# Queues by kind for waiting VectorE work, a new order of the first loads and folds, and the MLP scale on x instead of W1

## The chip, the cores and the metric

The kernel runs on the 8 NeuronCores of one Trainium2 chip, without collectives: each core computes half of the 32 tiles of 128 tokens of one batch element. The metric is the device time of the slowest core in microseconds (us). The engines are TensorE (PE, matmuls into PSUM), VectorE (DVE), ScalarE (ACT, the exp), GpSimd (POOL, which also issues the weight loads) and SyncE (SP, which issues the other transfers).

## The reference

One decoder block on x of 4 x 4096 x 1024, cut to what matters:

```python
xn = rmsnorm(x, norm_mix_g)
u = xn @ w_in                              # conv gates and values, q, k, v, branch gates
y_a = short_gated_conv(b_g, c_g, v_a, conv_w) @ w_a_out    # causal, 3 taps
# 4 heads, two softmax maps each, ALiBi bias, causal:
p = softmax(q k^T / 8 + bias)              # (B, H, 2, 128, S)
o = (p[:, :, 0] - lam * p[:, :, 1]) @ v
y_b = (rmsnorm(o, subln_g) * (1 - lam_init)) @ w_b_out
x = x + (sigmoid(g_a) * y_a + sigmoid(g_b) * y_b) @ w_o
h = rmsnorm(x, norm_mlp_g) @ w_mlp_in
x = x + square(relu(h)) @ w_mlp_out
return rmsnorm(x, norm_final_g)
```

## The kernel before

A core owns 16 query tiles in four groups (g = 0 to 3) of 512 tokens, and needs K and V of all 4096 tokens, in eight blocks of 512 (blocks 0 to 3 are its own, 4 to 7 the other core's). The program is written as one list per engine: each recorded operation goes to the end of its engine's list and waits for what it reads and overwrites, so **the order in which the Python code records is the order in which each engine works**, and an engine that waits holds up everything behind it. A tile that is one buffer is waited for as a whole.

*Start.* POOL issues the loads of Wk and x of block 4 in four pieces, four token tiles of block 4 (`tok_pool`, the tensor `xs`), Wv, x of block 0 and Wq. `fold_gain` multiplies Wk, Wv and Wq by the norm's gain on VectorE. `stats` computes a block's 1/rms: four squares on ScalarE, then `rstd` (VectorE, POOL's power, VectorE). `bcast` spreads 1/rms of a block over all partitions by TensorE and copies it to the tile `R`, which scales Q, K of blocks 1 to 3, and the normalised x.

*Attention.* `pairs` holds the (group, head, key tile) steps: 4 heads of 4, 8, 12 and 16 steps. Step n issues the scores of step n+1 (`qk`, TensorE), their exp (`ex`, ScalarE, on the diagonal also two masks on VectorE), then P V of step n in two halves (`pv`). After each half `other` does one round of other work: it calls `run_deferred`, which takes waiting VectorE operations from the queue `bg`, and then, while `credit` is above zero, takes chunks from the list `W`. A chunk is a projection of 8 matmuls of 512 columns into PSUM bank 7, the only bank that chunks have here, and its evacuation; its weight is taken off the credit (0.5 per half step). The weights stand in `W`: 1 for a projection, 0 for a load or a statistics step. At a change of group `until(g)` runs all of `W` up to that group's mark at once.

*Waiting work.* `background` puts VectorE operations into `bg` with a tag: "conv" (four operations between the second and third projection of a convolution chunk, `fv` and `fb`), "head" (ten after a head: 1/l, differences, norm), "norm" (eight, which normalise x of a block in place, and a spill), "fold". `settle(tag)` records, at once, everything up to the last operation of that tag, in the order in which it came. `epilogue` at a head's end settles "head", then copies the accumulators out of banks 4 and 5 by VectorE and of bank 6 by ScalarE.

*End.* Gates and output projection (`G_list`) of the four groups, from x normalised, then the MLP in four blocks of 512 tokens: `m_load` transposes x from memory into `m_x2` (two buffers), 32 `m_in` chunks fill `h2`, eight `m_out` chunks add to x. W1 is scaled by the MLP norm's gain in 64 VectorE operations ("fold") while the last group's attention and the gates run.

The functions that the change touches, and what calls them:

## Time and profile before

| | us |
|---|---|
| median of 3 runs | 1317.37 (1315.82 to 1317.42) |
| profiled execution, its own time | 1320.41 |
| its span, first to last instruction, slowest core | 1318.9 |
| spans of the 8 cores | 1307.3 to 1318.9 |
| TensorE busy in the span | 1171.4 |
| VectorE, ScalarE, POOL busy | 487.3, 543.0, 89.7 |

The profile is of one execution on its slowest core. An engine's busy time says little by itself: what counts is, stage by stage, which wait ends last. TensorE's granted clock is 1 at 2.4 GHz and 0.5 at 1.2 GHz, and a mean over a stretch lies between.

### The profile page before, as it was taken

What the parts mean: (1) busy time and instruction counts of PE and PEld (TensorE: products, weight loads), DVE (VectorE), ACT (ScalarE), POOL (GpSimd) and SP (SyncE); (2) the same over time, 40 slices, a digit from 0 to 9 for tenths busy, and PEclk for the clock granted to TensorE, in tenths of its full rate; (3) what the DMA queues carried; (4) which work ended last, traced back from release to release, by engine and by line L of the source; (5) the groups of instructions that cost most, each with busy time, mean ns of one, the idle gap of its engine ahead of it and who ended that gap; (6) DMA issues with size and microseconds to landing.
All of it is one profiled execution on the core that took longest, in us unless ns stands there. A gap on an engine that the chain in (4) does not pass through costs nothing.

```text
span 1318.9 us, 20312 instructions; the slowest of 8 cores (1307.3 to 1318.9 us)
## 1 busy us (share of the span) xinstructions
PE 1171.4 (89%) x7010; PEld 560.4 (42%) x7010; DVE 487.3 (37%) x1107; ACT 543.0 (41%) x744; POOL 89.7 (7%) x148
## 2 busy tenths in 40 slices
PE   3886677987898898897889899999999999999996
PEld 1333243443454344453445344444444444444442
DVE  2446454445434554325252464432122122122212
ACT  1263265656656467675667132233023113212300
POOL 3111100000000000100000000020000000000000
PEclk8888888998899899999899999999999999999998
DMA  9965612313012551654613757099313013012001
GB/s 175 228 157 97 132 65 65 70 36 68 18 29 45 109 109 32 105 109 118 144 33 69 197 127 239 10 214 170 104 50 78 16 49 97 0 48 80 1 32 48
DMA packets 67412, 117.75 MB, mean 89 GB/s; under 512 B 37072, under 2 KB 39376, under 8 KB 66288
## 3 DMA queue, kind: packets, MB, share of 16 engines
q0 software_dynamic: 14544, 44.11, 20.7%
q1 hardware_dynamic: 52768, 72.34, 18.1%
q8 instruction: 59, 0.97, 0.3%
q14 instruction: 41, 0.34, 0.1%
HBM read 120.69 MB, written 29.36 MB: 114 GB/s over the span
## 4 chain that ended last, share of the span: by engine, by line
PE 78%; DVE 9%; DMA 4%; issue 4%; ACT 3%; POOL 1%; DVEq 0%; SPq 0%; ACTq 0%; POOLq 0%
PE ps_all L404 78%; ACT big L664 2%; DMA big<-wv 2%; DMA big<-xs 2%; DVE big L793 1%; DVE big L689 1%; DVE big L492 1%; DVE big L549 1%; POOL big L409 1%; DVE big L611 1%; DVE big L604 0%; DVE big L602 0%; POOL big L723 0%; DVE big L715 0%; DVEq L152 0%
## 5 line engine op out<-in xcount | busy, mean ns | idle before, releaser
L404 PE MATMUL ps_all<-big 128*128 128x512 bf16 (+2 forms) x7010 | 1171.4, 333 | 135.0 <-DVE big L611 24.1
L404 PEld LDWEIGHTS ps_all<-big 128*128 128x128 bf16 (+1 forms) x7010 | 560.4, 100 | 745.5 <-issue 284.1
L664 ACT ACTIVATE big<-ps_all,big 128x1024 bf16<-128x1024 f32 (+3 forms) x384 | 339.0, 926 | 167.3 <-PE ps_all L404 158.9
L889 ACT ACTIVATE big<-ps_all 128x512 bf16<-128x512 f32 x128 | 76.2, 597 | 134.0 <-PE ps_all L404 133.6
L890 DVE TENSOR_TENSOR big<-big 128x512 bf16<-128x512 bf16 x128 | 54.4, 425 | 152.6 <-ACT big L889 152.1
L906 ACT ACTIVATE big<-big 128x1024 bf16<-128x1024 f32 x16 | 16.9, 1057 | 208.3 <-DVE big L901 208.3
L901 DVE SCALAR_TENSOR_TENSOR big<-ps_all,big 128x512 f32<-128x512 f32 x32 | 24.0, 751 | 162.9 <-PE ps_all L404 162.9
L793 DVE SCALAR_TENSOR_TENSOR big<-big,ps_all 128x512 f32<-128x512 f32 x64 | 43.7, 686 | 97.0 <-PE ps_all L404 96.6
L782 ACT ACTIVATE big<-ps_all,big 128x512 f32<-128x512 f32 x64 | 43.5, 686 | 58.9 <-PE ps_all L404 57.0
L448 ACT ACTIVATE big<-big 128x1024 bf16<-128x1024 f32 x32 | 33.8, 1056 | 47.4 <-DMA big<-xs 46.8
L821 ACT ACTIVATE big<-big 128x1024 bf16<-128x1024 f32 x16 | 16.9, 1057 | 71.9 <-DVE big L816 71.9
L669 DVE TENSOR_TENSOR big<-big 128x256 bf16<-128x256 bf16 x64 | 18.6, 290 | 61.6 <-ACT big L664 61.1
L816 DVE SCALAR_TENSOR_TENSOR big<-ps_all,big 128x512 f32<-128x512 f32 x32 | 22.1, 691 | 50.1 <-PE ps_all L404 41.1
L549 DVE TENSOR_SCALAR big<-ps_all,big 128x512 bf16<-128x512 f32 x32 | 24.0, 750 | 44.1 <-PE ps_all L404 44.1
L908 POOL TENSOR_TENSOR big<-big 128x1 f32<-128x1 f32 x16 | 8.7, 543 | 413.5 <-DVE big L907 413.5
L409 POOL DMA_DIRECT2D big<-w x32 | 17.4, 550 | 280.4 <-PE ps_all L404 167.9
L595 DVE TENSOR_TENSOR big<-ps_all,big 128x512 f32<-128x512 f32 x16 | 11.0, 690 | 49.7 <-PE ps_all L404 49.7
L671 DVE TENSOR_SCALAR big<-big 128x256 bf16<-128x256 bf16 x64 | 18.3, 286 | 29.2 <-ACT big L664 29.1
L723 POOL TENSOR_TENSOR big<-big 128x4 f32<-128x4 f32 x16 | 16.4, 1024 | 175.2 <-DVE big L721 175.1
L1051 DVE TENSOR_SCALAR big<-big 128x512 bf16<-128x512 bf16 x64 | 22.5, 352 | 4.3 <-DVE big L1051 0.9
L707 DVE SCALAR_TENSOR_TENSOR big<-big 128x128 f32<-128x128 f32 x64 | 22.3, 349 | 4.5
L796 DVE TENSOR_TENSOR big<-big 128x512 bf16<-128x512 f32 x32 | 22.1, 692 | 3.3
(65 smaller groups left out, 308.1 us busy)
## 6 DMA issues: line engine op xcount, KB each, us to landing
big<-xs SPq DMA_DIRECT2D x40, 512.0 KB, 9.1
big<-w POOLq DMA_DIRECT2D x32, 512.0 KB, 10.6
xm_sp<-big SPq DMA_DIRECT2D x16, 512.0 KB, 5.6
big<-xm_sp SPq DMA_DIRECT2D x16, 512.0 KB, 5.2
out<-big SPq DMA_DIRECT2D x16, 512.0 KB, 2.6
big<-xT POOLq DMA_DIRECT2D x24, 256.0 KB, 5.1
big<-xs POOLq DMA_DIRECT2D x8, 512.0 KB, 20.4
xn_sp<-big SPq DMA_DIRECT2D x4, 1024.0 KB, 4.5
```

What stands on the lines that cost most here:

```text
L404: S.op("pe", lambda e: e.matmul(out, lhsT, rhs, start=start, stop=stop, skip_group_check=skip), reads, writes)
L409: S.dma("pool", lambda e: e.dma_start(out=dst, in_=src), writes=bufs, extra=[S.last["pe"]] if paced else (), part=part)
L448: act(lambda e: e.activation(junk.ap, xt.ap, AF.Square, accum_out=ss1[blk].ap[:, t:t + 1]), [xt], [junk, ss1[blk]])
L549: dve(lambda e: e.tensor_scalar_mul(v_all[:, :, n, 0:128], ps.rearrange("p (h v) -> p h v", h=4), rs1[blk].ap[:, t:t + 1]), [key, rs1[blk] ...
L664: act(lambda e, a=a, b=b, c=c, s=s, PT=PT, scale=scale: e.activation(PT.ap[:, :, a:b], Sb[s][:, :, a:b], AF.Exp, bias=ccol(C_BTAB + c), sc ...
L707: dve(lambda e, t=t: e.scalar_tensor_tensor(o[:, 0, t, 0:128], o[:, 0, t, 0:128], rl[:, 0, t:t + 1], o[:, 1, t, 0:128], ALU.mult, ALU.add) ...
L782: act(lambda e: e.activation(t.ap, ps, AF.Tanh, bias=hbg.ap[:, 8 * w + dm:8 * w + dm + 1], scale=0.5), [key, hbg], [t])
L793: dve(lambda e: e.scalar_tensor_tensor(t.ap, t.ap, 1.0, ps, ALU.add, ALU.mult), [key, t], [t])
L889: act(lambda e: e.activation(r.ap, ps, AF.Relu), [key], [r])
L890: dve(lambda e: e.tensor_tensor(h2[fc].ap, r.ap, r.ap, ALU.mult), [r], [h2[fc]])
L901: dve(lambda e: e.scalar_tensor_tensor(x.ap[:, hs], ps, r2q[b].ap[:, t:t + 1], x.ap[:, hs], ALU.mult, ALU.add), [key, x, r2q[b]], [x])
L1051: return lambda: dve(lambda e: e.tensor_scalar_mul(W1[k].ap[:, c, :], W1[k].ap[:, c, :], ccol(C_GMLP + c)), [W1[k], cst], [W1[k]])
```

## The change

- `R` gets two buffers, and the queue "norm" becomes "norm0" and "norm1" (even and odd blocks).
- `bg` is one queue per tag. `run_deferred` takes from the first that is not empty, in the order conv, head, norm0, norm1, fold; two at a time where more than 10 wait (before: more than 8). `settle(tag)` empties that queue alone.
- `epilogue` copies bank 4, bank 6, bank 5, all on VectorE.
- Start: Wv and x of block 0 are loaded before the token tiles of block 4; 40 dummy matmuls run before the first projection and 16 after it (`warm`); the folds of Wv come before the statistics of block 4; all eight folds of Wq come after K of block 0; the four Q projections of block 0 are made first and evacuated after `bcast(0)`; the statistics of block 5 and of the halo move into the attention stage.
- `bcast` of blocks 1, 2 and 3 weighs 1 (before 0.2 or 0.6), `halo_norm` 1 (0.2), a halo chunk 0.5 (0.4).
- The 64 folds of W1 go. `m_fold` scales the eight slices of `m_x2` instead, eight for block 0 in the gates of the last group, the others between the `m_out` chunks of the block before. `m_load(0)` comes 12 rounds earlier.

```diff
-    R_b = ar.take("R", [512], F32)
+    R_b = [ar.take("R%d" % k, [512], F32) for k in range(2)]
...
-            settle("norm")
+            settle("norm%d" % (blk % 2))
...
-            background("norm", [nrm(k) for k in range(8)] + [spill])
+            background("norm%d" % (blk % 2), [nrm(k) for k in range(8)] + [spill])
...
+        def out(m):
+            dve(lambda e: e.tensor_copy(o[:, m, 0:3, 0:129], bank(4 + m)[:, 0:390].rearrange(
                 "p (t e) -> p t e", t=3)[:, :, 0:129]), [pk(4 + m)], [o_raw])
-        act(lambda e: e.copy(o[:, :, 3, 0:129], bank(6)[:, 0:260].rearrange(
+        out(0)
+        dve(lambda e: e.tensor_copy(o[:, :, 3, 0:129], bank(6)[:, 0:260].rearrange(
             "p (m e) -> p m e", m=2)[:, :, 0:129]), [pk(6)], [o_raw])
+        out(1)
...
-        for k in range(2 if len(bg) > 8 else 1):
-            if bg:
-                bg.pop(0)[1]()
-
-    bg = []
+        n = sum(len(q) for q in bg.values())
+        for k in range(2 if n > 10 else 1):
+            for q in bg.values():
+                if q:
+                    q.pop(0)()
+                    break
+
+    bg = {t: [] for t in ("conv", "head", "norm0", "norm1", "fold")}
 
     def background(tag, fns):
 
-        bg.extend((tag, f) for f in fns)
-
-    def settle(tag=None):
-
-        last = [k for k, (t, f) in enumerate(bg) if tag in (None, t)]
-        for k in range(last[-1] + 1 if last else 0):
-            bg.pop(0)[1]()
+        bg[tag].extend(fns)
+
+    def settle(tag):
+
+        while bg[tag]:
+            bg[tag].pop(0)()
...
+    def m_fold(b, c):
+        if b < 4:
+            x2 = m_x2[b % 2]
+            dve(lambda e: e.tensor_scalar_mul(x2.ap[:, c, :], x2.ap[:, c, :], ccol(C_GMLP + c)), [x2, cst], [x2])
...
+    def warm(n):
+
+        for k in range(n):
+            mm(bank(7)[:, 0:256], ident, cbf.ap, True, True, [cbf], [pk(7)])
+
+
+    warm(40)
...
+    warm(16)
+    for c in range(8):
+        fold_gain(Wv, c)
...
-    W += spread(ks(0) + vs(0), [lambda c=c: fold_gain(Wq, c) for c in range(8)])
-    W[-12:-12] = [(0, f) for f in stats(0, 5)]
-    W += [(0.2, bcast(0))]
-    W += spread(qs(0), xT_steps(1, 0) + stats(5, 1))
+    W += [(1, f) for f in ks(0)] + [(0, lambda: [fold_gain(Wq, c) for c in range(8)])]
+    W += [(0, f) for f in stats(0, 5)] + [(1, f) for f in vs(0)]
+
+    def q_first():
+        ps = [q_mm(0, h) for h in range(4)]
+        bcast(0)()
+        for h in range(4):
+            q_evac(0, h, *ps[h])
+    W += [(4, q_first)] + [(0, f) for f in xT_steps(1, 0)]
     mark(0)
-    W += spread(ks(5) + vs(5), stats(1, 2) + normed(0) + wc_load(0))
-    W += [(0.2, bcast(1))]
+    W += spread(ks(5) + vs(5), stats(5, 1) + [halo_stat] + stats(1, 2) + wc_load(0) + normed(0))
+    W += [(1, bcast(1))]
...
-    W += [(0.2, halo_norm)] + [(0.4, halo_chunk(ch)) for ch in range(4)]
-    W += spread(conv(0), normed(1) + stats(6, 3))
-    W += [(0.6, bcast(2))]
+    W += [(1, halo_norm)] + [(0.5, halo_chunk(ch)) for ch in range(4)]
+    W += spread(conv(0), stats(6, 3) + normed(1))
+    W += [(1, bcast(2))]
...
-        def fold(k):
-            def one(c):
-                return lambda: dve(lambda e: e.tensor_scalar_mul(W1[k].ap[:, c, :], W1[k].ap[:, c, :],
-                                                                 ccol(C_GMLP + c)), [W1[k], cst], [W1[k]])
-            return lambda: background("fold", [one(c) for c in range(8)])
...
-    deferred.append((36, lambda: m_load(0)))
+    deferred.append((24, lambda: m_load(0)))
+    deferred.append((48, lambda: background("fold", [lambda c=c: m_fold(0, c) for c in range(8)])))
...
             m_out(b, t, 0)
+            m_fold(b + 1, 2 * t)
             if pend:
                 m_fin2(pend.pop(0))
             if t + 2 < 4:
                 m_xload(T + 2)
             m_out(b, t, 1)
+            m_fold(b + 1, 2 * t + 1)
```

What this does to the order of work shows best on VectorE. In the rows below, `ps_all` is PSUM, `big` is the one SBUF tensor from which all tiles are cut, and x2 means that the row comes twice in a row. The first place is the second `bcast`, in the attention of the first group. Before (line 492 normalises x of block 0, 689 are copies at a head's end, 549 an evacuation of V, 669 and 671 masks, 484 the copy to `R`, 531 K times `R`):

```order
L492 SCALAR_TENSOR_TENSOR big<-big 128x512
L689 COPY big<-ps_all 128x3x129 x2
L492 SCALAR_TENSOR_TENSOR big<-big 128x512 x2
L549 TENSOR_SCALAR big<-ps_all,big 128x4x128
L669 TENSOR_TENSOR big<-big 128x2x128
L671 TENSOR_SCALAR big<-big 128x2x128
L492 SCALAR_TENSOR_TENSOR big<-big 128x512 x4
L484 COPY big<-ps_all 128x512
L531 TENSOR_TENSOR big<-ps_all,big 128x512
```

And after, at the same `bcast` (696 and 699 copies at a head's end, 705 to 724 the head's waiting operations, 551 V, 675 and 677 masks, 484 the copy to `R`, 533 K times `R`):

```order
L696 COPY big<-ps_all 128x3x129
L699 COPY big<-ps_all 128x2x129
L696 COPY big<-ps_all 128x3x129
L705 RECIPROCAL big<-big 128x8
L706 TENSOR_SCALAR big<-big 128x4
L551 TENSOR_SCALAR big<-ps_all,big 128x4x128
L675 TENSOR_TENSOR big<-big 128x2x128
L677 TENSOR_SCALAR big<-big 128x2x128
L709 TENSOR_TENSOR big<-big 128x4x128
L716 SCALAR_TENSOR_TENSOR big<-big 128x128 x2
L484 COPY big<-ps_all 128x512
L716 SCALAR_TENSOR_TENSOR big<-big 128x128 x2
```

The eight normalising operations (L492 before) are no longer ahead of the copy to `R`; what stands there is work of the head that has just ended, including the third copy, 128x2x129, which ScalarE made before.

The second place is a convolution chunk in the attention of the second group. Before (595 is `fv`, 599 to 604 the convolution between the projections, 611 `fb`, the evacuation at the chunk's end; 700 to 728 the head's operations, 721 and 728 behind POOL's power and product):

```order
L700 TENSOR_TENSOR big<-big 128x4x128
L707 SCALAR_TENSOR_TENSOR big<-big 128x128 x2
L595 TENSOR_TENSOR big<-ps_all,big 128x4x128
L707 SCALAR_TENSOR_TENSOR big<-big 128x128 x2
L715 SCALAR_TENSOR_TENSOR big<-big 128x128 x4
L721 TENSOR_SCALAR big<-big 128x4
L728 TENSOR_TENSOR big<-big 128x512
L599 COPY big<-big 128x4x2
L601 TENSOR_SCALAR big<-big 128x512
L602 SCALAR_TENSOR_TENSOR big<-big 128x512
L604 SCALAR_TENSOR_TENSOR big<-big 128x512
L611 TENSOR_TENSOR big<-ps_all,big 128x512
```

And after (601, 605 to 610 and 617 are the same operations of the convolution, 709 to 724 those of the head):

```order
L709 TENSOR_TENSOR big<-big 128x4x128
L716 SCALAR_TENSOR_TENSOR big<-big 128x128 x2
L601 TENSOR_TENSOR big<-ps_all,big 128x4x128
L605 COPY big<-big 128x4x2
L607 TENSOR_SCALAR big<-big 128x512
L608 SCALAR_TENSOR_TENSOR big<-big 128x512
L610 SCALAR_TENSOR_TENSOR big<-big 128x512
L617 TENSOR_TENSOR big<-ps_all,big 128x512
L716 SCALAR_TENSOR_TENSOR big<-big 128x128 x2
L724 SCALAR_TENSOR_TENSOR big<-big 128x128 x2
```

Between `fv` and `fb` stood the whole rest of the head; now only the four operations of the convolution do, and the head's follow `fb`.

The third place is the boundary between the first and the second block of the MLP. Before (901 are evacuations of `m_out`, 907 and 912 the final norm, 890 the square in an `m_in` chunk):

```order
L901 SCALAR_TENSOR_TENSOR big<-ps_all,big 128x512
L912 SCALAR_TENSOR_TENSOR big<-big 128x1024
L901 SCALAR_TENSOR_TENSOR big<-ps_all,big 128x512
L907 TENSOR_SCALAR big<-big 128x1
L890 TENSOR_TENSOR big<-big 128x512 x5
L912 SCALAR_TENSOR_TENSOR big<-big 128x1024
L890 TENSOR_TENSOR big<-big 128x512 x27
```

And after (917 evacuations of `m_out`, 890 now `m_fold`, 923 and 928 the final norm, 906 the square of `m_in`):

```order
L890 TENSOR_SCALAR big<-big 128x512
L923 TENSOR_SCALAR big<-big 128x1
L917 SCALAR_TENSOR_TENSOR big<-ps_all,big 128x512
L890 TENSOR_SCALAR big<-big 128x512
L928 SCALAR_TENSOR_TENSOR big<-big 128x1024
L917 SCALAR_TENSOR_TENSOR big<-ps_all,big 128x512
L890 TENSOR_SCALAR big<-big 128x512
L923 TENSOR_SCALAR big<-big 128x1
L906 TENSOR_TENSOR big<-big 128x512 x5
L928 SCALAR_TENSOR_TENSOR big<-big 128x1024
L906 TENSOR_TENSOR big<-big 128x512 x27
```

A fold now follows each evacuation of `m_out`; the last one, after the last evacuation, writes the tile that the first `m_in` matmul of the next block reads. On TensorE the change adds 56 dummy matmuls of 128x256 at the start and moves the Q projections of block 0 together.

## Rows read from the trace of the kernel before

**Rows 1.** Windows by stage: busy us of each engine (instructions), granted TensorE clock, DMA share, GB/s.

```profile
0.00:70.60 70.60, 44.62 (x172) 17.85 (x172) 23.23 (x56) 15.27 (x26) 18.26 (x37) 0.88 0.96 200
...
70.60:731.00 660.40, 555.77 (x4212) 284.92 (x4210) 293.34 (x729) 398.36 (x502) 50.84 (x74) 0.93 0.37 80
...
871.00:1319.00 448.00, 435.40 (x2018) 197.16 (x2015) 101.02 (x195) 95.28 (x162) 10.28 (x19) 0.99 0.27 66
```

**Rows 2.** What TensorE waited for: total us, times, longest us.

```profile
PE ps_all L404 <- DVE big L611: 24.1, 8, 4.7
```

**Rows 3.** Windows, columns as above: one after the halo, one after a head's end.

```profile
159.00:176.00 17.00, 11.51 (x128) 7.13 (x129) 5.61 (x23) 8.78 (x16) 1.04 (x1) 0.60 0.39 128
...
397.00:402.00 5.00, 3.47 (x17) 1.49 (x16) 2.03 (x6) 1.61 (x2) 0.00 (x0) 0.66 0.18 32
```

**Rows 4.** Timeline of the start: start us, us, operation, count, idle before it and releaser.

```profile
36.95 1.14 DVE L524 TENSOR_SCALAR big<-big 128x512 bf16<-128x512 bf16 x4 [1.55 <-DMA big<-wv]
...
56.14 1.06 ACT L448 ACTIVATE big<-big 128x1024 bf16<-128x1024 f32 x1 [0.73 <-DMA big<-xs]
...
58.97 0.69 DVE L529 CAST big<-ps_all 128x512 bf16<-128x512 f32 x1
...
59.57 0.35 DVE L524 TENSOR_SCALAR big<-big 128x512 bf16<-128x512 bf16 x1
...
60.69 0.74 DVE L549 TENSOR_SCALAR big<-ps_all,big 128x512 bf16<-128x512 f32 x1
...
64.38 0.68 DVE L484 COPY big<-ps_all 128x512 f32<-128x512 f32 x1
...
65.23 0.69 DVE L561 TENSOR_TENSOR big<-ps_all,big 128x512 bf16<-128x512 f32 x1 [0.17 <-PE ps_all L404]
...
70.61 4.52 ACT L664 ACTIVATE big<-ps_all,big 128x512 bf16<-128x512 f32 x6 [2.51 <-PE ps_all L404]
```

**Rows 5.** Timeline of the start: POOL's issues of four `xs` loads, and VectorE beside them.

```profile
5.87 2.18 POOL L409 DMA_DIRECT2D big<-xs  x4
...
33.90 2.16 POOL L409 DMA_DIRECT2D big<-xs  x4
...
34.15 1.25 DVE L524 TENSOR_SCALAR big<-big 128x512 bf16<-128x512 bf16 x4
```

**Rows 6.** Timeline at a convolution chunk of the second group.

```profile
208.45 0.69 DVE L728 TENSOR_TENSOR big<-big 128x512 bf16<-128x512 f32 x1 [1.32 <-POOL big L723]
...
211.72 0.69 DVE L611 TENSOR_TENSOR big<-ps_all,big 128x512 bf16<-128x512 f32 x1 [0.17 <-DVE big L604]
...
212.56 0.81 PE L404 MATMUL ps_all<-big 128*128 128x512 bf16 x3 [4.03 <-DVE big L611]
```

**Rows 7.** Timeline of TensorE at the second `bcast`.

```profile
111.99 1.44 PE L404 MATMUL ps_all<-big 128*128 128x512 bf16 x3 [2.17 <-DVE big L484]
```

**Rows 8.** Timeline of TensorE where the second group's first halo chunk starts.

```profile
162.39 0.59 PE L404 MATMUL ps_all<-big 128*128 128x32 bf16 x16 [6.10 <-DVE big L519]
```

**Rows 9.** Timeline of TensorE in the chunks run ahead of the second group.

```profile
144.59 1.89 PE L404 MATMUL ps_all<-big 128*128 128x512 bf16 x8 [1.01 <-DVE big L549]
```

**Rows 10.** Timeline at the end of a head of the third group.

```profile
394.59 0.56 DVE L689 COPY big<-ps_all 128x387 f32<-128x387 f32 x1
...
396.03 0.37 ACT L691 COPY big<-ps_all 128x258 f32<-128x258 f32 x1 [1.74 <-DVE big L689]
...
397.15 0.69 DVE L700 TENSOR_TENSOR big<-big 128x512 f32<-128x512 f32 x1
...
398.59 1.86 PE L404 MATMUL ps_all<-big 128*128 128x512 bf16 x4 [1.53 <-DVE big L561]
```

**Rows 11.** The page, part 5, and VectorE's timeline at the end of an MLP block.

```profile
L1051 DVE TENSOR_SCALAR big<-big 128x512 bf16<-128x512 bf16 x64 | 22.5, 352 | 4.3 <-DVE big L1051 0.9
...
974.99 0.75 DVE L901 SCALAR_TENSOR_TENSOR big<-ps_all,big 128x512 f32<-128x512 f32 x1 [4.96 <-PE ps_all L404]
```

**Rows 12.** Timeline of TensorE at a head's end in the fourth group.

```profile
610.14 2.40 PE L404 MATMUL ps_all<-big 128*128 128x512 bf16 x6 [4.70 <-DVE big L793]
```

More of the change, by code:

```diff
@@ L530, in k_evac @@
         else:
[L531 removed]
+            r = R_b[blk % 2]
+            dve(lambda e: e.tensor_tensor(dst.ap, ps, r.ap, ALU.mult), [key, r], [dst])
     def k_chunk(blk, h):
@@ L552, in v_chunk, with q_mm, q_evac @@
         return f
-    def q_chunk(g, h):
-        def f():
-            x = XT[slot_of[g]]
-            ps, key = obank()
-            for c in range(8):
-                mm(ps, Wq[c].ap[:, h * 128:(h + 1) * 128], x[c].ap, c == 0, c == 7, [Wq[c], x[c]], [key])
-            dst = qt_of[g % 2][h]
-            dve(lambda e: e.tensor_tensor(dst.ap, ps, R_b.ap, ALU.mult), [key, R_b], [dst])
-        return f
+    def q_mm(g, h):
+        x = XT[slot_of[g]]
+        ps, key = obank()
+        for c in range(8):
+            mm(ps, Wq[c].ap[:, h * 128:(h + 1) * 128], x[c].ap, c == 0, c == 7, [Wq[c], x[c]], [key])
+        return ps, key
+    def q_evac(g, h, ps, key):
+        dst, r = qt_of[g % 2][h], R_b[g % 2]
+        dve(lambda e: e.tensor_tensor(dst.ap, ps, r.ap, ALU.mult), [key, r], [dst])
+    def q_chunk(g, h):
+        return lambda: q_evac(g, h, *q_mm(g, h))
     def halo_chunk(ch):
@@ L943, in build_program @@
     slot_of[4], slot_of[0], slot_of[5] = 0, 1, 2
-    for t in range(4):
-        tok_pool(4, t)
     for q in range(2):
@@ L949, in build_program @@
         wload(XT[1], xT_d[0], 4 * q, 4, 512)
+    for t in range(4):
+        tok_pool(4, t)
     for q in range(2):
@@ L963, in build_program @@
         k_evac(4, h, *ps4[h])
+    warm(16)
+    for c in range(8):
+        fold_gain(Wv, c)
     for f in stats(4, None):
@@ L969, in build_program @@
         wload(XT[2], xT_d[5], 4 * q, 4, 512)
-    for c in range(8):
-        fold_gain(Wv, c)
     def wc_load(ch):
@@ L999, in build_program @@
     W += spread(conv(1), xT_steps(3, 1) + stats(7, None))
-    W += [(0.6, bcast(3))]
+    W += [(1, bcast(3))]
     W += spread(ks(3) + vs(3) + qs(3), xT_steps(7, 0))
@@ L1047, in w1_steps @@
             out += pieces([W1[k]], w1_d, 4096 * k, 4096)
-        def fold(k):
-            def one(c):
-                return lambda: dve(lambda e: e.tensor_scalar_mul(W1[k].ap[:, c, :], W1[k].ap[:, c, :],
-                                                                 ccol(C_GMLP + c)), [W1[k], cst], [W1[k]])
-            return lambda: background("fold", [one(c) for c in range(8)])
-        return [(2 + 4 * n, f) for n, f in enumerate(out)] + [(26 + 4 * n, fold(2 * h + n)) for n in range(2)]
+        return [(2 + 4 * n, f) for n, f in enumerate(out)]
     def w2_load(f0, n):
@@ L1098, in build_program @@
     run_deferred(True)
-    settle()
+    for t in bg:
+        settle(t)
     w2_load(0, 18)
```

14 lines of the change are left out of this document (6 added, 8 removed).

## The prediction

> **What bounds the kernel now.** I first read the windows by stage, to see where TensorE is not working. In the MLP it is busy 435.4 of 448.0 us at a granted clock of 0.99: nothing to win there but its end [rows 1]. The attention stage (70.6 to 731 us) is busy 555.8 of 660.4 us at a mean clock of 0.93, so 104.6 us are idle, and the clock takes more. With two levels of clock (1.2 and 2.4 GHz), a mean of 0.93 over the busy time costs 0.07 x 555.8 = 38.9 us. VectorE is busy for 293 us of that stage and ScalarE for 398, so neither is full: TensorE waits for an engine that does the wrong thing first, not for one with too much to do. The start (0 to 70.6 us) is different: the DMA engines are busy 0.96 of it.
>
> Next I read the list of what TensorE waited for. Its longest line is the evacuation that ends a convolution chunk, 24.1 us in eight waits, one of them 4.7 [rows 2]. Last I read the granted clock behind such waits: it is 0.60 in the 17 us after the halo and 0.66 in the 5 us after a head's end [rows 3]. The chip lowers the clock after TensorE has stood, so each long wait is paid a second time.
>
> **The start.** The Wv load moves ahead of the four `xs` loads of block 4; the bytes and the queue are the same, so the last load that the first exp needs, `xs` of block 0, should still arrive at about 56 us [rows 4]. The chain behind it is VectorE's: from 58.97 it runs two K casts (0.69), then four V evacuations with six folds of Wq in between (0.74 and 0.35), and reaches the copy of `R` at 64.38; then each Q chunk is evacuated as TensorE makes it, and the first exp starts at 70.61 [rows 4]. In the changed order the casts and folds stand ahead of the statistics, and the 32 Q matmuls ahead of the copy of `R`. What is left behind 58.97 is four V evacuations at a pitch of 0.66 (0.74 less some 0.08, as neighbours overlap: the fold at 59.57 starts 0.60 after a cast of 0.69), the copy 0.68, one Q evacuation 0.69 and some 0.5 us to the exp: 58.97 + 2.6 + 0.7 + 0.7 + 0.5 = 63.5, a gain of 7.1. The cover is TensorE's: V of block 4, K, V and Q of block 0 are 128 matmuls, some 28 us at the full clock (435.4 us / 2018 in the MLP is 0.216 each [rows 1]), and Wv arrives earlier than the 36.95 of the row. (The 2.1 MB that it passes are 10 us at the 200 GB/s of [rows 1]; I take 6, as the other loads are under way at the same time.) So they end near 60. The dummy matmuls cost nothing: 40 run before the first weights are there, 16 in a stretch in which TensorE waited for Wv anyway. If the clock is low through half of these matmuls they end 6 us later and the gain is about 2; without any wait it is 9. I take 7.
>
> Here a rule speaks against the change. The issue of four `xs` loads by POOL took 2.18 us with VectorE nearly idle and 2.16 us with four bf16 folds of 1.25 us running beside it [rows 5]. So the eight folds of Wq in one block, beside which POOL issues loads, cost those loads nothing that the row shows. The Trainium skill, page "SBUF — State Buffer", section "SBUF: two separate sides", says that a DMA issued from POOL cannot have its descriptors written while VectorE runs in a two-port mode. By that rule those issues would wait for the folds, and this trace does not show it. What it would give is among the rivals.
>
> **The queues.** Before, a convolution chunk that is settled drags every head operation queued ahead of it onto VectorE: in the row, the normalisation that waits for POOL (208.45) and the four convolution operations run before the evacuation at 211.72, and TensorE stands 4.03 us [rows 6]. After, the convolution operations go first and the head's follow the evacuation. What stays of each of the eight waits is about the evacuation and its hand-over, 0.69 + 0.2: 24.1 - 8 x 0.9 = 17 us [rows 2, 6]. The work is not gone, it is moved behind; the next place it could be late is the following head's end, four or more pairs on. Bounds: 10, if diagonal pairs still hold VectorE for their masks, and 22. The second and fourth `bcast` no longer wait for eight normalising operations, as `R` has two buffers: TensorE stood 2.17 us for the copy [rows 7], twice is 4 (2 to 6).
>
> **The halo.** TensorE stood 6.10 us in front of the first halo chunk, which shares a slot with `halo_norm` and needs its result [rows 8]. With a slot of its own, pair work comes between; an ordinary head's end still costs about 3, so 3.2 is won (1.5 to 6). The larger weights also leave about one more chunk each to be run ahead at the start of the second and third group, where one bank is shared and TensorE stands 1.01 us per chunk [rows 9]: minus 2 (0 to 3).
>
> **The head's end.** Before, two copies, ScalarE's copy, and with more than eight operations queued both the reciprocal and the 0.69 us product stand before the chunk's evacuation, for which TensorE stands 1.53 us [rows 10]. After, VectorE does all three copies (the third is a 258-wide piece, between 0.37, ScalarE's price, and 0.56, that of 387 columns), which ends the last copy about when ScalarE's ended; the product mostly moves behind the evacuation. That is worth 0.6 at about 8 of 16 heads: 5 (0 to 10).
>
> **The MLP scale.** 64 folds of W1 at 0.352 go, 22.5 us of VectorE [rows 11]; where they stood before the head's copies and a gate's evacuation, TensorE stood 4.70 us [rows 12]. About 3 of that and 2 at two later heads: 5 (2 to 8). In their place 32 folds of x2 come. Eight are hidden behind block 3's gates, 21 of the others behind the matmuls of `m_out`, but the last of each of three blocks stands behind the last evacuation, and the next block's first matmul reads the same tile. TensorE, which runs on there now [rows 1], must wait 0.75 + 0.352 and two hand-overs, about 1.25 [rows 11]: minus 3.7 (3.3 to 5).
>
> **The clock.** Of 38.9 us I let 16 come back, those behind the waits that go (the halo's window alone holds 0.40 x 11.51 = 4.6, a head's end 0.34 x 3.47 = 1.2) [rows 1, 3]. Bounds: 6, if ordinary head ends and the groups' starts still lower it, and 30.
>
> **Sum.** 7 + 17 + 4 + 3.2 - 2 + 5 + 5 - 3.7 + 16 = 51.5 us. The profiled execution took 1320.4 us, so 1268.9; the runs' median is 3.0 lower, so I say 1265 to 1266. The lower bounds together give 15.5 (2 + 10 + 2 + 1.5 - 3 + 0 + 2 - 5 + 6), the upper 87.7.
>
> **Rivals.**
> - *The stalls move.* The chunks have one PSUM bank, and VectorE's copies, masks and evacuations are the same number; if the waits return behind the masks, 15 to 30 us are left, about 1294. For it: VectorE is only 44% busy in the stage and TensorE waits for it all the same [rows 1]. Against: in the row the late work is none that TensorE needs [rows 6].
> - *More.* If the clock stays up from the second group on, its term is 30, the head's end gives its 10 and the queues their 22: 30 - 16 + 10 - 5 + 22 - 17 = 24 more, about 1242.
> - *Slower.* ScalarE's copy is put on the engine that TensorE waits for at every head's end [rows 10]. If it is fully exposed, 0.43 + 0.17 x 16 heads is 9.6 us, and if then every head end lowers the clock as in [rows 3], another 16 x 1.2 = 19, together 29. It decides from the point where the queues, `bcast` and clock give back less than 20 of their 37 and the head's end nothing: the rest is 7 + 3.2 - 2 + 5 - 3.7 = 9.5. With none of the 37, the time is up to 1337; I say 1325.
> - *It does not do what it says.* If the queues seldom hold two kinds at a time, little is reordered, and start, MLP and run-ahead nearly cancel (7 - 3.7 - 2): about 1316. The eight waits speak against.
> - *POOL held up.* If folds hold back the issues, `xs` of block 0 comes 8 x 0.35 = 2.8 us later, and the time is about 1268. This is what the page "SBUF — State Buffer" of the Trainium skill would do here.
>
> **Chances.** Forecast (35 to 75 us gained) 0.58, stalls move 0.25, more 0.08, slower 0.05, no effect 0.03, POOL 0.01. A difference of under 0.2% (2.6 us) cannot be told from none, so faster is 0.92, same 0.03, slower 0.05. For eight in ten the range takes the forecast, the lower end of "more" as far as 1240, and nearly all of the stalls that move (1287 to 1302): 1240 to 1302.
>
> **What the profile after would show.** First exp at 63 to 64 us, not after 66; TensorE's waits for the convolution's evacuation under 8 us together, none over 2; no wait of 2 us at the second `bcast`, none over 4 at the halo; the attention stage under 620 us at a clock of 0.95 or more; three new waits of 1 to 1.4 us in the MLP, at the blocks' ends. I am wrong if the idle time of the attention stage stays near 100 us, or if it falls and the clock does not rise.

## The result, and the profile after

The changed kernel takes 1285.65 us (median of 4 runs, 1285.20 to 1287.45) against 1317.39, a ratio of 0.9764 with an interval of 0.9747 to 0.9781: 2.2 to 2.5% less, about 32 us. A second set of runs of the changed kernel, the control of the experiments, has a median of 1286.05 and gave 0.9753 (0.9735 to 0.9772). The forecast was 1265 in a range of 1240 to 1302: the right sign, and 0.6 of the size.

The windows of the profiled execution of the changed kernel, split where the first exp starts, where the last one starts, and where the MLP starts (busy us of PE, PEld, DVE, ACT, POOL, then granted clock, DMA share, GB/s):

```profile
0.00:66.99 66.99, 49.55 (x226) 24.06 (x226) 21.44 (x56) 10.69 (x18) 18.31 (x37) 0.95 0.92 187
66.99:688.40 621.41, 545.71 (x4193) 284.90 (x4194) 285.55 (x697) 395.23 (x493) 51.06 (x74) 0.95 0.39 86
688.40:831.00 142.60, 136.64 (x630) 61.23 (x629) 68.74 (x123) 36.76 (x60) 10.48 (x18) 0.99 0.59 153
831.00:1283.70 452.70, 436.40 (x2020) 197.23 (x2018) 106.33 (x216) 94.15 (x160) 10.29 (x19) 0.99 0.25 65
```

And the attention stage of the trace before, cut at the same events:

```profile
70.60:726.00 655.40, 552.62 (x4193) 283.48 (x4192) 289.33 (x717) 396.83 (x500) 50.84 (x74) 0.93 0.37 80
```

Almost all of the gain lies in the attention stage: 621 us instead of 655. The start gives 3.6, the gates 3.4 (146.0 before; on the median core nothing, 140.4 before and 140.8 now), and the MLP, 446.9 before, loses 5.8 (2.6 on the median core). The clock in the attention stage is 0.95 instead of 0.93.

What TensorE waited for in the whole changed execution (us, times, longest), and five rows of the same view of before that are not shown above:

```profile
PE ps_all L404 <- DVE big L696: 16.0, 26, 2.1
PE ps_all L404 <- DVE big L804: 15.9, 20, 4.4
PE ps_all L404 <- DVE big L551: 8.4, 8, 2.3
PE ps_all L404 <- DVE big L617: 6.8, 4, 2.6
PE ps_all L404 <- DVE big L890: 3.8, 3, 1.3
PE ps_all L404 <- DVE big L699: 3.5, 13, 0.3
PE ps_all L404 <- DVE big L578: 1.4, 1, 1.4
PE ps_all L404 <- DVE big L484: 1.2, 1, 1.2
PE ps_all L404 <- DVE big L520: 0.4, 1, 0.4
```

```profile
PE ps_all L404 <- DVE big L793: 17.5, 20, 4.7
PE ps_all L404 <- ACT big L691: 9.7, 11, 0.9
PE ps_all L404 <- DVE big L689: 8.7, 10, 2.8
PE ps_all L404 <- DVE big L484: 4.5, 3, 2.2
PE ps_all L404 <- DVE big L572: 2.1, 2, 1.2
```

By these lists the evacuation at a convolution chunk's end (L611 before, L617 now) costs 6.8 us instead of 24.1 [rows 2]. The list names the operation that ended last before TensorE went on, and that is not always the one that it waited for. In 175 of the 183 waits for VectorE in the two traces TensorE starts 0.145 to 0.148 us after the named operation ends. In the other eight it starts sooner, and each time an evacuation had ended 0.146 us before. One of them, in the changed kernel:

```profile
189.95 0.69 DVE L617 TENSOR_TENSOR big<-ps_all,big 128x512 bf16<-128x512 f32 x1 [0.17 <-DVE big L610]
190.56 0.19 DVE L705 RECIPROCAL big<-big 128x8 f32<-128x8 f32 x1
190.79 1.71 PE L404 MATMUL ps_all<-big 128*128 128x512 bf16 x4 [1.99 <-DVE big L705]
```

Here TensorE starts 0.04 us after the reciprocal and 0.15 after the evacuation, so the wait is the evacuation's. Counted so, a chunk's end costs 10.0 us in six waits instead of 27.6 in ten.

The `bcast` copy (L484) costs 1.2 us instead of 4.5; the halo (`halo_norm` L520 and the halo chunk L578 now, L519 [rows 8] and L572 before) 1.8 instead of 8.2. The copies at a head's end (L696 and L699 now, L689 and L691 before) cost 19.5 instead of 18.4: nothing was won there. The gates' evacuation (L804 now, L793 before) hardly moved, and L890, the fold of x2, is new.

For the comparisons below one table was worked out from the traces. In the attention stage (first to last exp), the distance from each matmul's start to the next is split in three: its columns at the full clock, what they take more at the granted clock, and the rest. The score matmuls have 64 rows and start in pairs 3 ns apart; a pair is counted once. At the full clock 512 columns take 0.216 us (the MLP's row [rows 1]), at the half 0.427. The rest is waiting, and also some 0.1 us before and after the score matmuls of every step, which all the kernels have; so its differences count, not its level. The numbers are medians over six cores; the other two lack some matmul records. The columns come to 458 to 459 us in every row. The runs `q1_fifo`, `h1_act`, `m1_w1fold` and `m2_early` shared a chip on which some cores ran at a lower clock, in the kernel before as well (1328.7 us there), so of these four the stages of the undisturbed cores are read (four or five in the table for the first and the third) rather than the time.

| kernel | stage | rest | lost to the clock |
|---|---|---|---|
| before | 653.7 | 162.1 | 31.6 |
| changed | 621.2 | 139.1 | 23.4 |
| changed, control | 621.6 | 139.4 | 23.8 |
| changed, one queue | 653.6 | 162.6 | 32.4 |
| before, queues alone | 632.0 | 149.0 | 22.5 |
| changed, one R | 634.8 | 148.7 | 27.1 |
| changed, old weights | 618.0 | 139.0 | 19.8 |
| changed, ScalarE's copy as before | 618.0 | 140.0 | 19.4 |
| changed, folds of W1 | 626.0 | 142.6 | 25.0 |
| changed, folds of x2 earlier | 622.2 | 139.1 | 24.3 |
| changed, old start | 618.6 | 138.0 | 20.3 |
| changed, ScalarE beside VectorE | 610.0 | 133.6 | 18.4 |
| three edits | 607.4 | 131.2 | 17.4 |

### The profile page after: what moved, and what is told of

The parts are those of the page before. It is cut to its first block, busy times and chain, and to the rows that moved or that the text cites. A ratio compares the mean times of both kernels' runs of the same rounds, so it can differ in the third digit from the quotient of the medians.

```text
span 1283.7 us, 20390 instructions; the slowest of 8 cores (1268.7 to 1283.7 us)
## 1 busy us (share of the span) xinstructions
PE 1168.3 (91%) x7066; PEld 567.4 (44%) x7066; DVE 482.1 (38%) x1091; ACT 536.8 (42%) x728; POOL 90.1 (7%) x148
## 4 chain that ended last, share of the span: by engine, by line
PE 80%; DVE 7%; ACT 4%; issue 4%; DMA 3%; POOL 1%; SPq 0%; DVEq 0%; ACTq 0%; POOLq 0%
PE ps_all L404 80%; ACT big L670 3%; DMA big<-xs 3%; DVE big L696 1%; DVE big L804 1%; ACT big L448 1%; POOL big L409 1%; DVE big L699 1%; DVE big L551 0%; DVE big L565 0%; DVE big L608 0%; DVE big L610 0%; DVE big L617 0%; SPq L836 0%; DVE big L493 0%
## 5 line engine op out<-in xcount | busy, mean ns | idle before, releaser
L404 PE MATMUL ps_all<-big 128*128 128x512 bf16 (+6 forms) x7066 | 1168.3, 331 | 102.9 <-DVE big L696 16.0
L404 PEld LDWEIGHTS ps_all<-big 128*128 128x128 bf16 (+2 forms) x7066 | 567.4, 100 | 703.3 <-issue 226.7
L804 DVE SCALAR_TENSOR_TENSOR big<-big,ps_all 128x512 f32<-128x512 f32 x64 | 43.8, 686 | 102.5 <-PE ps_all L404 102.1
L793 ACT ACTIVATE big<-ps_all,big 128x512 f32<-128x512 f32 x64 | 43.4, 685 | 59.3 <-PE ps_all L404 59.2
L409 POOL DMA_DIRECT2D big<-w x32 | 17.6, 557 | 283.5 <-PE ps_all L404 163.0
L551 DVE TENSOR_SCALAR big<-ps_all,big 128x512 bf16<-128x512 f32 x32 | 23.4, 749 | 34.1 <-PE ps_all L404 34.0
L601 DVE TENSOR_TENSOR big<-ps_all,big 128x512 f32<-128x512 f32 x16 | 11.1, 691 | 34.4 <-PE ps_all L404 34.4
L493 DVE SCALAR_TENSOR_TENSOR big<-big 128x512 bf16<-128x512 bf16 x32 | 23.0, 743 | 0.0
```

The lines of the kernel that those rows point to most:

```text
L404: S.op("pe", lambda e: e.matmul(out, lhsT, rhs, start=start, stop=stop, skip_group_check=skip), reads, writes)
L409: S.dma("pool", lambda e: e.dma_start(out=dst, in_=src), writes=bufs, extra=[S.last["pe"]] if paced else (), part=part)
L493: dve(lambda e: e.scalar_tensor_tensor(x[k].ap, x[k].ap, ccol(C_GMIX + k), r.ap, ALU.mult, ALU.mult), [x[k], cst, r], [x[k]])
L551: dve(lambda e: e.tensor_scalar_mul(v_all[:, :, n, 0:128], ps.rearrange("p (h v) -> p h v", h=4), rs1[blk].ap[:, t:t + 1]), [key, rs1[blk] ...
L793: act(lambda e: e.activation(t.ap, ps, AF.Tanh, bias=hbg.ap[:, 8 * w + dm:8 * w + dm + 1], scale=0.5), [key, hbg], [t])
L804: dve(lambda e: e.scalar_tensor_tensor(t.ap, t.ap, 1.0, ps, ALU.add, ALU.mult), [key, t], [t])
```

## The experiments

Theory: the queue is the change; without it an evacuation for which TensorE stands carries the rest of a head on its back, and the clock follows. Rival: the gain is a sum of independent parts, each about as large as the prediction has it.

**One queue again** (`q1_fifo`), on the changed kernel:

```diff
-        n = sum(len(q) for q in bg.values())
-        for k in range(2 if n > 10 else 1):
-            for q in bg.values():
-                if q:
-                    q.pop(0)()
-                    break
+        for k in range(2 if len(bg) > 8 else 1):
+            if bg:
+                bg.pop(0)[1]()
...
-        while bg[tag]:
-            bg[tag].pop(0)()
+        last = [k for k, (t, f) in enumerate(bg) if tag in (None, t)]
+        for k in range(last[-1] + 1 if last else 0):
+            bg.pop(0)[1]()
```

> The changed kernel with one queue in order of arrival again (two at a time above 8), all else kept. If the queues are the main term, as the prediction has it: TensorE's waits for the evacuation that ends a convolution chunk go from 6.8 us back to 20 or more, the clock loses some 6 us on top, and the time is 1306 to 1314 us. Rival: the gain came from the halo's slot, the second R and the order of the steps, and the order within the queue counts little: under 1294.

Measured: 1331.7 us, ratio 1.0028 (0.9995 to 1.0062), so nothing of the gain is left. That is more than the theory asked for. (The edit also takes the threshold for two at a time back from 10 to 8; the two are not told apart, here and in the next run.) The timeline of this kernel at a convolution chunk (start, length, idle before and what ended it):

```profile
304.48 0.17 DVE L730 TENSOR_SCALAR big<-big 128x4 f32<-128x4 f32 x1
304.80 1.01 POOL L732 TENSOR_TENSOR big<-big 128x4 f32<-128x4 f32 x1 [38.82 <-DVE big L730]
305.97 0.69 DVE L737 TENSOR_TENSOR big<-big 128x512 bf16<-128x512 f32 x1 [1.32 <-POOL big L732]
306.85 0.49 DVE L607 TENSOR_SCALAR big<-big 128x512 f32<-128x512 f32 x1
309.25 0.69 DVE L617 TENSOR_TENSOR big<-ps_all,big 128x512 bf16<-128x512 f32 x1 [0.17 <-DVE big L610]
310.08 2.72 PE L404 MATMUL ps_all<-big 128*128 128x512 bf16 x6 [6.63 <-DVE big L617]
```

The head's end (L730, POOL's power, L737) stands ahead of the convolution (L607 and on), VectorE itself waits 1.32 us for POOL, and TensorE stands 6.63 us for an evacuation of 0.69. On core 6 these waits make 20.8 us by the list, longest 6.7, and with three under other names 27.2 in ten waits, against 27.6 in ten before the change. In the table the rest rises by 23.2 us and the clock's loss by 8.6, together the 32 of the stage, which is back at its length before.

**The queues alone** (`p1_queues`), on the kernel before: the same lines the other way round, and

```diff
-    bg = []
+    bg = {t: [] for t in ("conv", "head", "norm", "fold")}
```

> The kernel before with the queues by kind alone (conv, head, norm, fold; two at a time above 10), all else as before. From the run with one queue, which gave back all of the gain: queues alone win about 30 us, 1285 to 1290, with the waits at the ends of the convolution chunks under 8 us. Rival, the prediction's sum (17 for these waits and a share of the clock's 16, the rest by the other parts): 1294 to 1300.

Measured: 1300.26 us, 0.9867 (0.9846 to 0.9888): 17.5 us less, the rival's value; the slowest core decides that, and the median core gains more. The stage shrinks by 21.7, 13.1 of it the rest and 9.1 clock. So the queue's part is 32 us in the attention stage when it is taken from the changed kernel, and 22 there when it is put on the kernel before. What holds it back there, in what TensorE waited for:

```profile
PE ps_all L404 <- DVE big L484: 7.1, 3, 5.5
PE ps_all L404 <- DVE big L519: 5.3, 1, 5.3
```

The wait for the `bcast` copy has grown, from 4.5 to 7.1: with convolution and head ahead of them, the normalising operations wait longer, and with one R all that are left must be done before the copy. The halo's wait is the old one, as the weights are the old ones. A third place does not show in these two rows, because the list puts it under L721:

```profile
177.93 5.38 DVE L492 SCALAR_TENSOR_TENSOR big<-big 128x512 bf16<-128x512 bf16 x8
183.23 0.68 DVE L611 TENSOR_TENSOR big<-ps_all,big 128x512 bf16<-128x512 f32 x1
184.06 1.44 PE L404 MATMUL ps_all<-big 128*128 128x512 bf16 x3 [4.31 <-DVE big L721]
```

Eight normalising operations of the next block stand ahead of a convolution chunk's last evacuation: with one queue "norm" the chunk's projection settles them, though it reads the block before. (The longest of the eight waits before, 4.7 us, has the same eight ahead of it.) With this wait and two more that the list puts under L443 the chunks' ends cost 11.1 us in six waits, not under the 8 that was expected.

**One R** (`r1_oneR`), on the changed kernel:

```diff
-    R_b = [ar.take("R%d" % k, [512], F32) for k in range(2)]
+    R_b = [ar.take("R", [512], F32)] * 2
...
-            settle("norm%d" % (blk % 2))
+            settle("norm")
...
-            background("norm%d" % (blk % 2), [nrm(k) for k in range(8)] + [spill])
+            background("norm", [nrm(k) for k in range(8)] + [spill])
...
-    bg = {t: [] for t in ("conv", "head", "norm0", "norm1", "fold")}
+    bg = {t: [] for t in ("conv", "head", "norm", "fold")}
```

> The changed kernel with one buffer R and one queue "norm", the other queues kept. The prediction's term is 4 us (two waits of 2.17): 1290. Rival, from the run with the queues alone, where TensorE stood 5.5 us at the second bcast: 6 to 10 us slower than the changed kernel, the clock behind that wait included, 1292 to 1296. Third: the normalisation is seldom still queued there, within 2 us.

Measured: 1297.02 us, 0.9838 (0.9819 to 0.9857), 11 us slower than the control: the rival. Timeline at the `bcast` of block 2:

```profile
215.33 4.72 DVE L493 SCALAR_TENSOR_TENSOR big<-big 128x512 bf16<-128x512 bf16 x7
220.22 0.69 DVE L484 COPY big<-ps_all 128x512 f32<-128x512 f32 x1 [0.17 <-DVE big L493]
221.06 1.44 PE L404 MATMUL ps_all<-big 128*128 128x512 bf16 x3 [4.51 <-DVE big L484]
```

Seven normalising operations in a row, then the copy, and TensorE stands 4.51 us. The waits for L484 are 9.5 us instead of 1.2, the clock's loss 3.3 more. Before the change this wait was 2.17 [rows 7]; with the queues by kind alone it is 5.5, and the second R is what keeps them from that.

**The old weights** (`w1_weights`):

```diff
-    W += [(1, bcast(1))]
+    W += [(0.2, bcast(1))]
...
-    W += [(1, halo_norm)] + [(0.5, halo_chunk(ch)) for ch in range(4)]
+    W += [(0.2, halo_norm)] + [(0.4, halo_chunk(ch)) for ch in range(4)]
...
-    W += [(1, bcast(2))]
+    W += [(0.6, bcast(2))]
...
-    W += [(1, bcast(3))]
+    W += [(0.6, bcast(3))]
```

> The changed kernel with the old weights (bcast 0.2 and 0.6, halo_norm 0.2, a halo chunk 0.4). The prediction's terms (halo 3.2 won, chunks run ahead 2 lost): 1.2 us slower, 1287. Rival, from the run with the queues alone (5.5 us of waiting at the halo, and a lower clock behind it): 4 to 6 us slower, 1290 to 1292, with that wait back.

Measured: 1281.91 us, 0.9722 (0.9698 to 0.9745): 4 us faster than the control, with intervals that overlap at their ends. Both expectations missed. The halo's wait is back in what TensorE waited for,

```profile
PE ps_all L404 <- DVE big L520: 5.4, 1, 5.4
```

and the stage is no longer for it: the rest is the same to 0.4 us, so the new weights pay elsewhere what they win here. By the waits that is at the chunks' ends (6.5 us with the old weights, 10.0 with the new) and at the copies of a head's end (17.2 and 19.5). The 4 us are the clock's, and the runs below show that this term moves by as much without a cause that the table names.

**ScalarE's copy as before** (`h1_act`): VectorE copies banks 4 and 5, then ScalarE bank 6.

```diff
-        out(0)
-        dve(lambda e: e.tensor_copy(o[:, :, 3, 0:129], bank(6)[:, 0:260].rearrange(
+        for m in range(2):
+            dve(lambda e, m=m: e.tensor_copy(o[:, m, 0:3, 0:129], bank(4 + m)[:, 0:390].rearrange(
+                "p (t e) -> p t e", t=3)[:, :, 0:129]), [pk(4 + m)], [o_raw])
+        act(lambda e: e.copy(o[:, :, 3, 0:129], bank(6)[:, 0:260].rearrange(
             "p (m e) -> p m e", m=2)[:, :, 0:129]), [pk(6)], [o_raw])
-        out(1)
```

> The changed kernel with ScalarE's copy of bank 6 at a head's end, behind VectorE's two, as before. The prediction's step (a head's end wins 5 us): 1290. Rival, from the two traces (waits for the copies 18.4 us before, 21.5 after): the copy on VectorE costs what it saves, and the time is 1282 to 1287; then the waits for banks 4, 5 and 6 together stay within 3 us of 21.5.

Measured: 1283.94 us; the stage is 618.0, the rest 140.0 against 139.4. The rival: the copy on VectorE wins nothing. The waits for the three banks are 20.7 us (11.6 for ScalarE's, 9.1 for VectorE's) against 19.5 in the changed kernel; the 21.5 of the expectation counts the reciprocal's 2.0, which is a chunk's end.

**ScalarE beside VectorE** (`h2_par`): ScalarE's copy is recorded first and has a dependence of its own.

```diff
+        act(lambda e: e.copy(o[:, :, 3, 0:129], bank(6)[:, 0:260].rearrange(
+            "p (m e) -> p m e", m=2)[:, :, 0:129]), [pk(6)], ["o3"])
+        for m in range(2):
+            dve(lambda e, m=m: e.tensor_copy(o[:, m, 0:3, 0:129], bank(4 + m)[:, 0:390].rearrange(
+                "p (t e) -> p t e", t=3)[:, :, 0:129]), [pk(4 + m)], [o_raw])
...
-            dve(lambda e: e.reciprocal(rl.unsqueeze(3), o[:, :, :, 128:129]), [o_raw], [est])
+            dve(lambda e: e.reciprocal(rl.unsqueeze(3), o[:, :, :, 128:129]), [o_raw, "o3"], [est])
```

> The changed kernel with bank 6 copied at a head's end by ScalarE, beside VectorE's two copies and not behind them (a dependence of its own for that piece). If TensorE waits there for the third copy in a row on VectorE: the waits for banks 4, 5 and 6 fall from 21.5 us to about 12 and the time is 8 to 14 us less than the control, 1272 to 1278. Rival: ScalarE comes late from its exps, and TensorE waits for it instead: within 2 us of the control.

Measured: 1270.86 us, 0.9649 (0.9631 to 0.9668), 13.7 us less than the control. First the timeline of the changed kernel at a head's end, then that of this one:

```profile
218.03 0.55 DVE L696 COPY big<-ps_all 128x387 f32<-128x387 f32 x1
218.73 0.33 PE L404 MATMUL ps_all<-big 128*128 128x129 bf16 x3 [1.13 <-DVE big L696]
218.75 0.43 DVE L699 COPY big<-ps_all 128x258 f32<-128x258 f32 x1 [0.17 <-DVE big L696]
219.28 0.56 DVE L696 COPY big<-ps_all 128x387 f32<-128x387 f32 x1
219.32 0.22 PE L404 MATMUL ps_all<-big 128*128 128x129 bf16 x1 [0.27 <-DVE big L699]
219.99 0.39 PE L404 MATMUL ps_all<-big 128*128 128x129 bf16 x4 [0.45 <-DVE big L696]
```

```profile
208.19 0.37 ACT L694 COPY big<-ps_all 128x258 f32<-128x258 f32 x1
209.27 0.56 DVE L697 COPY big<-ps_all 128x387 f32<-128x387 f32 x1
209.97 0.39 PE L404 MATMUL ps_all<-big 128*128 128x129 bf16 x4 [1.14 <-DVE big L697]
210.00 0.56 DVE L697 COPY big<-ps_all 128x387 f32<-128x387 f32 x1 [0.17 <-DVE big L697]
210.71 0.39 PE L404 MATMUL ps_all<-big 128*128 128x129 bf16 x4 [0.35 <-DVE big L697]
```

TensorE waits three times in a row in the first (1.13, 0.27, 0.45), twice in the second, and the third copy is off VectorE: ScalarE made it a microsecond before the first of the others. The waits for the copies fall from 19.5 to 13.8 us, the rest by 5.8 and the clock's loss by 5.4. In the kernel before, ScalarE had stood idle 1.74 us for VectorE's copies [rows 10], because all three pieces were written to one tile that is waited for as a whole; no limit of the engines asked for that. Against `h1_act`, which differs in the dependence and the order alone, the stage is 8.0 us shorter, 6.4 of it the rest. The Trainium skill, page "PSUM — Partial Sum Buffer", section "Specifications (TRN2)", says that ScalarE and VectorE can read PSUM at the same time as long as they use different banks. The run agrees where it can be seen: at two of the 16 head ends copies of the two engines overlap (from 97.20 and 97.23 us on core 7), and there too they take 0.37 to 0.38 and 0.56 to 0.57 us.

**Folds of W1 instead of x2** (`m1_w1fold`): the 64 folds of W1 are queued as "fold" again, and the calls of `m_fold` go.

```diff
-        return [(2 + 4 * n, f) for n, f in enumerate(out)]
+        return [(2 + 4 * n, f) for n, f in enumerate(out)] + [(26 + 4 * n, fold(2 * h + n)) for n in range(2)]
...
-    deferred.append((24, lambda: m_load(0)))
-    deferred.append((48, lambda: background("fold", [lambda c=c: m_fold(0, c) for c in range(8)])))
+    deferred.append((36, lambda: m_load(0)))
...
-            m_fold(b + 1, 2 * t)
...
-            m_fold(b + 1, 2 * t + 1)
```

> The changed kernel with the folds of W1 back and without those of x2. The prediction's step (5 won at the heads' ends, 3.7 lost at the blocks' ends): 1287, with the three waits of 1.3 us at the MLP's blocks gone. Rival, from the two traces (waits at the chunks of the last group's stage 15.5 us before, 14.4 after): the folds of W1 cost 1 to 2 us only, so it is 1283 to 1284.

Measured: 1288.49 to 1303.26 us, too wide for these terms. On cores 5 to 7 the attention stage is 4 us longer than in the table's control (626.0 against 621.6; 3 of it the rest, 1 the clock), the gates 2 longer than on the median core of the changed kernel, and the MLP 4 shorter. So the folds of W1 cost 5 to 6 us, near the prediction's 5, and the net is near its 1.3; the rival's 1 to 2 us was too low. Terms of this size lie near the scatter of the clock's loss, so this is an estimate from a few cores.

**Folds of x2 earlier** (`m2_early`):

```diff
-            m_fold(b + 1, 2 * t)
+            if t < 2:
+                for c in range(4 * t, 4 * t + 4):
+                    m_fold(b + 1, c)
...
-            m_fold(b + 1, 2 * t + 1)
```

> The changed kernel with the folds of x2 four after each of the first half evacuations of the first two token tiles, none behind the block's last evacuation. If the three waits of 1.26 us at the blocks' ends come from the fold that stands last: they go, and the time is 3.8 us less, 1282. Rival: the wait is for the evacuation of m_out itself and stays: 1285 to 1286.

Measured: 1281.50 us, with no idle time at the blocks' ends; the MLP of the median core takes 446.7 us, 5 less than in the changed kernel, and the attention stage is as long. The same place in the changed kernel, and then in this one:

```profile
935.51 0.75 DVE L917 SCALAR_TENSOR_TENSOR big<-ps_all,big 128x512 f32<-128x512 f32 x1 [4.70 <-PE ps_all L404]
936.18 0.34 DVE L890 TENSOR_SCALAR big<-big 128x512 bf16<-128x512 bf16 x1
936.67 0.59 PE L404 MATMUL ps_all<-big 128*128 128x512 bf16 x2 [1.27 <-DVE big L890]
```

```profile
929.72 12.46 PE L404 MATMUL ps_all<-big 128*128 128x512 bf16 x57
```

**The old start** (`s1_start`): loads, folds, statistics and Q projections in the order before, no dummy matmuls.

```diff
-    warm(40)
...
-    warm(16)
-    for c in range(8):
-        fold_gain(Wv, c)
     for f in stats(4, None):
         f()
+    for c in range(8):
+        fold_gain(Wv, c)
...
-    W += [(4, q_first)] + [(0, f) for f in xT_steps(1, 0)]
...
+    W += [(0.2, bcast(0))]
+    W += spread(qs(0), xT_steps(1, 0) + stats(5, 1))
```

> The changed kernel with the start as before: order of the first loads, folds and statistics, no dummy matmuls, Q projections after the copy of R, the statistics of block 5 and of the halo where they were. If the gain of the start passes through to the end: first exp at 69 to 70 us on the median core and 6 us more, 1291 to 1292. Rival: the statistics that no longer stand in the attention stage give that stage back as much, so within 2 us of the control.

Measured: 1290.77 us, 0.9796 (0.9770 to 0.9821), 5.7 slower than the control, with intervals that just touch; that is what was expected if the start's gain passes through to the end. First exp at 68.7 us on the median core, 62.9 in the control. By the table the old start gives 3 us back in the attention stage, about what the clock's loss falls by (3.5).

**No dummy matmuls** (`n1_nowarm`):

```diff
-    warm(40)
...
-    warm(16)
```

> The changed kernel without its 56 dummy matmuls. The prediction's price is nothing, and if they win nothing either: within 2 us of the changed kernel, first exp at 62 to 64 us on the median core. Rival: without them the first projections run at the lower clock, 28 matmuls and more at 0.43 instead of 0.22 us, and the first exp comes 2 to 6 us later.

Measured: 1286.49 us, 0.9763 (0.9748 to 0.9779), first exp at 62.9 us on the median core in both. They cost nothing and win nothing.

**Three edits** (`b1_best`): ScalarE beside VectorE, the early folds, and

```diff
-        for k in range(2 if n > 10 else 1):
+        for k in range((2 if n > 10 else 1) if waiting or bg["head"] else 0):
...
-        run_deferred()
+        run_deferred(waiting=amount > 0)
```

> The changed kernel with three edits: ScalarE copies bank 6 beside VectorE's two copies; the folds of x2 stand after the first four half evacuations; in the half step ahead of a head's end no waiting operation other than the last head's is taken, so that none stands ahead of the copies. The first alone won 13 to 15 us, the second some 4, the third should win 0.7 us at 8 to 12 of 16 heads: 1259 to 1264. Rival: what is not taken there is recorded at once ahead of the next evacuation that needs it, and the third wins nothing: 1266 to 1268.

Measured: 1266.84 us, 0.9621 (0.9601 to 0.9642), 4 us under `h2_par`. That is what the early folds alone explain; the third edit wins nothing that can be told (the rival): the attention stage is 2.6 us shorter than in `h2_par`, less than the scatter of the clock's loss. This version beats the changed kernel by 1.4% and the one before by 3.8%.

## Why the prediction was right, and where not

Its terms beside what the profile after shows, in us:

| term | forecast | measured |
|---|---|---|
| start | 7 | 3.6 (slowest core), 6 on the median core |
| convolution's queue | 17 | 17.6 (17.3 by the list) |
| `bcast` | 4 | 3.3 |
| halo | 3.2 | 6.4 |
| chunks run ahead | -2 | -1.2 |
| head's end | 5 | -1.1 |
| folds of W1 | 5 | 1.6 at the gates' evacuation |
| folds of x2 | -3.7 | -3.8 |
| clock | 16 | 10.0 |
| sum | 51.5 | 36.4, of 35.2 of the two profiled times |

(The chunks run ahead: waits for V and Q evacuations in the attention stage, 9.9 before, 11.1 after. Clock: 8.2 in the attention stage of the median core, 1.8 in the gates of the slowest; that of the start is in its term.)

**Right.** The mechanism, and its largest term to 0.6 us. Of the signs that were named, the three waits at the MLP's boundaries came out (1.3 us each), and no wait of 2 us is left at the second `bcast` and none of 4 at the halo. The idle time that the prediction read as 104.6 us is 75.7 by the windows (621.41 less 545.71), and the clock rose with it to 0.95. Three signs miss: the stage's 621 us are not under 620; the waits at the chunks' ends are 6.8 us by the list but 10.0 counted as above, not under 8, and one is 2.6; the first exp of the slowest core comes after 66 us (63.1 on the median core).

**Wrong, the head's end.** The step said that VectorE ends the last copy about when ScalarE's ended, and that the moved product is worth 0.6 at eight heads. The third copy is 0.43 us and serial, the waits rose by 1.1, and taking the edit back changed the rest by 0.6. That is 6 of the 16 us that are missing. The row was at hand: in [rows 10] ScalarE's copy waited for VectorE, and the question was why.

**Wrong, the start's cover.** The step said that the matmuls end near 60. The slowest core:

```profile
45.20 0.17 DVE L443 TENSOR_SCALAR big<-big 128x4 f32<-128x4 f32 x1 [12.41 <-ACT big L448]
46.77 2.73 DVE L551 TENSOR_SCALAR big<-ps_all,big 128x512 bf16<-128x512 f32 x4
47.67 16.51 PE L404 MATMUL ps_all<-big 128*128 128x512 bf16 x72 [2.28 <-DVE big L551]
57.47 1.06 ACT L448 ACTIVATE big<-big 128x1024 bf16<-128x1024 f32 x1 [0.75 <-DMA big<-xs]
60.31 2.73 DVE L551 TENSOR_SCALAR big<-ps_all,big 128x512 bf16<-128x512 f32 x4
64.29 0.69 DVE L484 COPY big<-ps_all 128x512 f32<-128x512 f32 x1 [1.26 <-PE ps_all L404]
66.99 3.19 ACT L670 ACTIVATE big<-ps_all,big 128x512 bf16<-128x512 f32 x4 [8.37 <-DVE big L565]
```

V of block 4 needs the statistics of block 4, whose token tiles now come behind Wv and x of block 0. The four V evacuations start at 46.77, TensorE stands 2.28 us for the first, goes on at the lower clock (0.50 granted from 47.67 to 51.00, eight matmuls), and ends at 64.2; VectorE waits 1.26 us for it at the copy of R. (The step's price for a low clock was itself wrong: half of 128 matmuls at 0.427 instead of 0.216 us end 13.5 us later, not 6.) What was moved back in the load queue was late one stage earlier than the step looked. No issue by POOL fell beside the folds of Wq, so the rival of POOL held up remains untried here.

**Mis-sized, the clock** (6 of the missing us). The step took the missing share of the clock times the busy time, 38.9 us, as lost, and let 16 come back, two fifths. Counted matmul by matmul 31.6 were lost in that stage, and 8.2 came back, a quarter. **Mis-sized, the folds of W1** (3 by the wait alone, though `m1_w1fold` lengthens the two stages by 5 to 6) **and the halo** (3 too low by the waits; but `w1_weights` shows that the weights behind it win nothing in all).

**The rivals.** "The stalls move" gave 1294, and the 1285.65 lie nearer to that than to the forecast. Its mechanism is not what the changed kernel shows: of the 66.9 us in which TensorE waits for VectorE in the attention stage the masks fill 3.3, of the 85.2 before 4.2. But a stall that moves is what happens to half of the change: with the queues and one R the stall does move, from the convolution's chunk to `bcast` (9.5 us of waits). "Slower" was right in that VectorE's copy costs a head's end; its price is 1.1 us in waits, not 9.6. The parts were treated as a sum, and are not one: taken from the changed kernel, queues and second R are worth 32 to 36 us (by the stage, by the ratio) and 11; the queues alone are worth 17.5. Why the other parts bring nothing at all under one queue is argued from the waits of `q1_fifo`, not shown part by part.

## What to carry to other kernels

Where an engine works in order and another waits for some of its operations, put those first, and then ask at once what is starved by it and which buffer makes someone wait for the starved work: the two edits belong together. When an engine on the list of waits is released by another engine at a drain of the same kind, look whether the data or only the tile's name ties them; splitting the dependence was worth more here (8 us of the stage against `h1_act`) than moving the copy, which won nothing. A loop's last write into the tile that the next loop reads first costs a full hand-over, and can be moved earlier for nothing.
